# First expert table: a shorter list of candidate pairs, a fourth row buffer, and gate matrices built in groups of four from unit 40 to unit 123

## The chip, the cores and the metric

The kernel runs on one core of a Trainium2 chip. The metric is device microseconds from start to end of one execution; the median of three runs counts. The engines are TensorE (PE, matrix products; PEld is its weight load), VectorE (DVE), ScalarE (ACT), GpSimd (POOL) and SyncE (SP), which here only issues transfers. The engines run their own programs and meet at semaphores.

## The reference

One layer of a decoder: a mixer (retention and gated linear attention), then a PEER block, in which every token picks 16 experts per head out of 128 x 128 by product keys. Only the PEER block matters here:

```
s1 = einsum('thd,hnd->thn', q[:, :, 0], sub_keys1)      # 8 heads, 128 first keys
s2 = einsum('thd,hnd->thn', q[:, :, 1], sub_keys2)      # 128 second keys
v1, i1 = top_k(s1, 16)
v2, i2 = top_k(s2, 16)
cand_s = (v1[..., :, None] + v2[..., None, :]).reshape(128, 8, 256)
cand_i = (i1[..., :, None] * 128 + i2[..., None, :]).reshape(128, 8, 256)
top_s, sel = top_k(cand_s, 16)
eidx = take_along_axis(cand_i, sel, axis=-1)
gate = softmax(top_s, axis=-1)
act = gelu(einsum('thkd,td->thk', u_tab[eidx], xb))
return einsum('thk,thkd->td', gate * act, v_tab[eidx])
```

There are 512 prompt tokens and 64 sample tokens, 2048 features and 16384 experts, all in float32.

## The kernel before

The program runs stages one after the other: input projection, mixer, output projection, queries, `experts_hidden` (the first expert table, `u_tab`), `outputs` (the second table, `v_tab`), `finish`. The change touches `experts_hidden` alone, from 1506 to 2920 us of the profiled execution.

**Two ways to the experts.** 384 of the tokens (`ND`) take the dense way: the whole table goes by, one unit of 128 experts after another (`NKEYS` = 128 units of 1 MB), PE multiplies each unit with all 384 tokens (48 matmuls of 128x384, L1612 to L1614: three products for a split in two parts), ACT applies gelu (L1668) and SP stores the result to `hidden`. Which of these products count is said by gate matrices, one 128x128 matrix per token, that the next stage multiplies in. The other 192 tokens take the sparse way: for each of 192 columns (`NGATHER`) POOL gathers 128 table rows of 8 KB with an indirect transfer (L1540, 1 MB each), and DVE forms the dot products with the tokens (`dot`, L1803).

**One unit on each engine.** SP loads the unit after next (`Units.load`); it may go once `split_lo` of the unit that had this buffer is done. ACT makes the high part (`split_hi`, L1401) once PE has finished the unit before the last, DVE the low part (`split_lo`, L1405), PE multiplies. In its iteration n DVE does `split_lo(n+1)`, then one piece of routing (`route`, n < 40) or the scaled one-hot rows of the gate matrices (`firsts_hots`), then its dots.

**Routing, units 0 to 39.** The tokens form five tiles, eight units to a tile. In them DVE finds the best 16 of 128 keys for 16 lists (`best_keys`, three units), adds all 16 x 16 = 256 pairs per head (`candidates`), takes the best 16 of them with MAX8, FIND_INDEX8 and MATCH_REPLACE8 (`best_pairs`, two units; five passes over each head's list), turns the index into two positions with a shift and a mask and looks the keys up (`first_keys`, `pick`, `softmax`, two units).

**Gate matrices, units 40 to 87.** A gate matrix is the product of two 128x128 matrices of one-hot rows: POOL makes the second keys' (`hot[1]`, L1556), DVE the first keys' times the gates (`hot[0]`, L1811), PE multiplies them (L1597) after the unit's 48 matmuls, ACT copies four at a time to a staging buffer (L1653), and SP stores each 32 (`store_group`, 2 MB). Each unit makes `per_unit` = 8 of them, in two halves of `B` = 4, so that 384 are made in 48 units. There is one set of eight `hot` buffers: POOL and DVE wait until PE has made all eight of the unit before (`made`, 2m).

**Gathers.** A table of corners, `spread`, says how many gathers have been issued by which unit: 22 by unit 40, 114 by unit 88, 192 by unit 128. They start at unit 17. Three row buffers (`ROWS`) take turns, so gather g waits for dot g-3. In a unit, POOL issues the gathers first and makes `hot[1]` after them.

Of the kernel before, what the change touches and what calls it, by code (L numbers as in the profile page):

```python
# [62 lines left out]
ROWS = 3  # L63
AHEAD = 3
# [1361 lines left out]
def experts_hidden(nc, name, c, u_units, h_src, hidden, queries, keys, u_rows, h_rows, expert_ids, dots, gates0, G):  # L1426
# [17 lines left out]
    with ExitStack() as ctx:  # L1444
# [6 lines left out]
        row = [a.sb(f"row{s}", [P, D]) for s in range(ROWS)]  # L1451
# [3 lines left out]
        spare = a.sb("spare", [P, HEADS * C2])  # L1455
# [3 lines left out]
        cand_left = spare[:].rearrange("p (h n) -> p h n", n=C2)  # L1459
        picks_hot = spare[:].rearrange("p (k j) -> p k j", j=TOPK)  # L1460
        hot = [[spare[:, (2 * n + x) * P:(2 * n + x + 1) * P] for n in range(per_unit)] for x in range(2)]
# [7 lines left out]
        half = [a.sb(f"half{n}", [P, HEADS, TOPK], U32) for n in range(2)]  # L1469
# [18 lines left out]
        row_in = [a.gpsimd_dma_sem(f"row_in{s}") for s in range(ROWS)]  # L1488
# [3 lines left out]
        def _(sp):  # L1492
# [22 lines left out]
            for n in range(NKEYS):  # L1515
# [15 lines left out]
        def _(pool):  # L1531
# [3 lines left out]
            def gather(g):  # L1535

                wait(pool, row_used, g - ROWS + 1)

                pool.sem_inc(carried, 1)
                pool.indirect_dma_start(row[g % ROWS][:], None, u_rows,  # L1540
                                        bass.IndirectOffsetOnAxis(expert_ids[:, g:g + 1], 0)).then_inc(row_in[g % ROWS], 16)

            for n in range(NKEYS):
                if n == first_gate:
                    pool.wait_ge(kept, 3 * (TILES - 2))
                for g in gathers(n):
                    gather(g)
                m = n - first_gate
                if 0 <= m < ND // per_unit:

                    wait(pool, made, 2 * m)

                    pool.sem_inc(carried, 1)
                    for x in range(per_unit):
                        k = per_unit * m + x
                        nc.gpsimd.tensor_scalar(hot[1][x], iota[:], seconds[:, k:k + 1], None,  # L1556
                                                ALU.is_equal).then_inc(seconds_hot, 1)

        @block.tensor
        def _(pe):  # L1560
# [29 lines left out]
            def gate_matrices(m):  # L1590
                for y in range(2):

                    wait(pe, staged, 2 * (m - 1) + y + 1)
                    pe.wait_ge(seconds_hot, per_unit * m + B * (y + 1))
                    pe.wait_ge(firsts_hot, per_unit * m + B * (y + 1))
                    for x in range(B):
                        ins = mm(tq[y][:, x, :], hot[1][B * y + x], hot[0][B * y + x], start=True, stop=True)  # L1597
                    ins.then_inc(made, 1)
# [6 lines left out]
            for n in range(NKEYS):  # L1605
# [16 lines left out]
                if first_gate <= n < after_gates:  # L1622
                    gate_matrices(n - first_gate)

        @block.scalar
        def _(act):
# [17 lines left out]
            def stage_gates(m):  # L1644
                x, at = (m // 4) % 2, per_unit * (m % 4)
                if m % 4 == 0:

                    wait(act, g_stored[x], 16 * (m // 8))
                if m == 0:
# [597 lines left out]
```

## Time and profile before

| | us |
|---|---|
| median of 3 runs (4140.73 to 4147.33) | 4144.82 |
| the profiled execution | 4139.19 |
| its span, first to last instruction | 4137.4 |
| first table: gelu of unit 0 / unit 40 / unit 88 / unit 127 begin at | 1530.0 / 1956.8 / 2573.0 / 2916.8 |
| PE busy, of the span | 3629.7 |
| DVE busy, of the span | 2599.5 |
| POOL busy, of the span | 1261.4 |
| mean granted TensorE clock | 0.930 |

The profiled execution lies 5.6 us below the median and 1.5 us below the lowest of the three runs. Busy shares over the span are means over stages with different limits, so they say little on this stage. The beginnings of the gelus (one a unit, right after the unit's last matmul) divide the stage into units.

### The profile page before, as it was taken

How to read it: one execution, taken by the hardware profiler on the slowest of the kernel's cores; microseconds unless marked ns; L12 is line 12 of the kernel's file. 1: busy time of each engine (PE TensorE's matmuls, PEld its weight loads, DVE VectorE, ACT ScalarE, POOL GpSimd, SP SyncE). 2: the span in 40 equal slices, each digit the busy share in tenths (PEclk: the TensorE clock that was granted, in tenths of full speed). 3: DMA queues.
4: the chain of work that ended last, by engine and by line, in shares of the span. 5: the costliest groups of instructions: out<-in, count | busy, mean ns of one | idle time of the engine just before them, and what ended most of it. 6: DMA issues, size and time to landing. Idle time of an engine off the chain costs nothing. (4 is left out here: it accounts for less than half of the span.)

```text
span 4137.4 us, 49902 instructions
## 1 busy us (share of the span) xinstructions
PE 3629.7 (88%) x19469; PEld 3375.9 (82%) x19469; DVE 2599.5 (63%) x3484; ACT 1083.1 (26%) x984; POOL 1261.4 (30%) x990
## 2 busy tenths in 40 slices
PE   6999996876977969987888888999699999999996
PEld 5888885655856869877888888999699999999996
DVE  3111112883223129999766776777687888888887
ACT  3222222332112123322333333222122222222222
POOL 0000000000000000112988996333244444445441
PEclk8999997777988989998999999999899999999998
DMA  4222223534333454554777878999788898989986
GB/s 159 107 109 107 108 99 109 159 115 172 120 143 109 160 183 148 202 208 181 290 289 284 305 295 306 381 374 381 281 332 338 335 359 320 365 323 347 350 320 232
DMA packets 209787, 983.08 MB, mean 238 GB/s; under 512 B 20593, under 2 KB 84401, under 8 KB 111202
## 3 DMA queue, kind: packets, MB, share of 16 engines
q1 hardware_dynamic: 130898, 523.57, 34.1%
q0 software_dynamic: 60960, 424.18, 26.9%
q10 hardware_dynamic: 17776, 33.27, 2.2%
q8 instruction: 99, 1.62, 0.2%
q14 instruction: 54, 0.44, 0.0%
HBM read 873.43 MB, written 107.52 MB: 237 GB/s over the span
## 5 line engine op out<-in xcount | busy, mean ns | idle before, releaser
L1612 PE MATMUL hidden_hp<-hidden_dense_hi,hidden_whi 128*128 128x384 f32 x2048 | 713.2, 348 | 65.8 <-DVE hidden_wlo L1405 65.8
L2038 PE MATMUL outputs_vp<-outputs_w_hi,outputs_whi 128*128 128x384 f32 x2048 | 694.3, 339 | 81.7 <-DVE outputs_wlo L1405 41.6
L1613 PE MATMUL hidden_hp<-hidden_dense_lo,hidden_whi 128*128 128x384 f32 x2048 | 701.4, 343 | 0.0
L1614 PE MATMUL hidden_hp<-hidden_dense_hi,hidden_wlo 128*128 128x384 f32 x2048 | 700.7, 342 | 0.0
L2039 PE MATMUL outputs_vp<-outputs_w_lo,outputs_whi 128*128 128x384 f32 x2048 | 692.4, 338 | 0.0
L2040 PE MATMUL outputs_vp<-outputs_w_hi,outputs_wlo 128*128 128x384 f32 x2048 | 692.3, 338 | 0.0
L1540 POOL DMA_INDIRECT hidden_row<-u_rows,expert_ids x192 | 319.7, 1665 | 1220.6 <-DVEq L1782 713.4
L1803 DVE CUSTOM_DVE_ANT_0 hidden_row<-hidden_row,hidden_h_row 128x2048 f32<-128x2048 f32 x192 | 438.3, 2293 | 134.3 <-DMA hidden_row<-u_rows,expert_ids 133.1
L1853 POOL DMA_INDIRECT outputs_row<-v_rows,outputs_id x192 | 318.6, 1660 | 629.6 <-DVE accg L1987 572.9
L1401 ACT CAST outputs_whi<-outputs_raw 128x2048 fp32r<-128x2048 f32 x128 | 244.8, 1912 | 858.6 <-PE outputs_vp L2040 604.1
L2038 PEld LDWEIGHTS outputs_vp<-outputs_w_hi,outputs_whi 128*128 128x128 f32 x2048 | 390.9, 191 | 86.4 <-issue 78.0
L1612 PEld LDWEIGHTS hidden_hp<-hidden_dense_hi,hidden_whi 128*128 128x128 f32 x2048 | 399.6, 195 | 74.4 <-DVE hidden_wlo L1405 57.3
L1987 DVE SCALAR_TENSOR_TENSOR accg<-outputs_row,outputs_w_op,accg 128x2048 f32<-128x2048 f32 x192 | 450.5, 2347 | 3.7 <-DVE accg L1987 0.5
L1405 DVE TENSOR_TENSOR hidden_wlo<-hidden_raw,hidden_whi 128x2048 fp32r<-128x2048 f32 x128 | 296.2, 2314 | 190.6 <-ACT hidden_whi L1401 189.7
L1556 POOL TENSOR_SCALAR hidden_spare<-hidden_iota,hidden_seconds 128x128 f32<-128x128 f32 x384 | 400.7, 1057 | 7.6 <-PE hidden_tq L1597 6.1
L1613 PEld LDWEIGHTS hidden_hp<-hidden_dense_lo,hidden_whi 128*128 128x128 f32 x2048 | 398.9, 195 | 0.0
L1405 DVE TENSOR_TENSOR outputs_wlo<-outputs_raw,outputs_whi 128x2048 fp32r<-128x2048 f32 x128 | 293.1, 2290 | 167.4 <-ACT outputs_whi L1401 165.2
L1614 PEld LDWEIGHTS hidden_hp<-hidden_dense_hi,hidden_wlo 128*128 128x128 f32 x2048 | 397.3, 194 | 0.0
L2039 PEld LDWEIGHTS outputs_vp<-outputs_w_lo,outputs_whi 128*128 128x128 f32 x2048 | 390.8, 191 | 0.0
L2040 PEld LDWEIGHTS outputs_vp<-outputs_w_hi,outputs_wlo 128*128 128x128 f32 x2048 | 390.6, 191 | 0.0
L487 PE MATMUL in_proj_acc<-in_proj_whi,rows_hi 128*128 128x512 f32 x960 | 373.5, 389 | 0.0
L492 PE MATMUL in_proj_acc<-in_proj_wlo,rows_hi 128*128 128x512 f32 x768 | 298.8, 389 | 0.0
(308 smaller groups left out, 5058.9 us busy)
## 6 DMA issues: line engine op xcount, KB each, us to landing
hidden_raw<-u_units SPq DMA_DIRECT2D x128, 1024.0 KB
outputs_raw<-v_units SPq DMA_DIRECT2D x128, 1024.0 KB
w_in_raw<-w_in SPq DMA_DIRECT2D x48, 1024.0 KB, 5.5
hidden<-hidden_hid SPq DMA_DIRECT2D x128, 192.0 KB
gate_mat<-hidden_big SPq DMA_DIRECT2D x12, 2048.0 KB
outputs_w<-hidden SPq DMA_DIRECT2D x16, 1536.0 KB
outputs_g<-gate_mat SPq DMA_DIRECT2D x16, 1536.0 KB
w_out_raw<-w_out SPq DMA_DIRECT2D x16, 1024.0 KB, 6.1
```

The lines of the kernel that those rows point to most:

```text
L487: nc.tensor.matmul(acc[t][:], hi[:, kk, tok], whi[q][:, k, :], start=first, stop=False)
L1405: self.nc.vector.tensor_tensor(self.lo[s][:], self.raw[s][:], self.hi[s][:].bitcast(F32), ALU.subtract).then_inc(self.lo_done, 1)
L1540: pool.indirect_dma_start(row[g % ROWS][:], None, u_rows, bass.IndirectOffsetOnAxis(expert_ids[:, g:g + 1], 0)).then_inc(row_in[g % ROWS], 16)
L1556: nc.gpsimd.tensor_scalar(hot[1][x], iota[:], seconds[:, k:k + 1], None, ALU.is_equal).then_inc(seconds_hot, 1)
L1612: mm(o, un.hi[s][:, x, :], h_hi[:, x, :], start=x == 0, stop=False)
L1613: mm(o, un.hi[s][:, x, :], h_lo[:, x, :], start=False, stop=False)
L1614: ins = mm(o, un.lo[s][:, x, :], h_hi[:, x, :], start=False, stop=x == KT - 1)
L1803: v.tensor_tensor_reduce(r[:], r[:], h_row[g % 3 // 2][:], 1.0, 0.0, mult, ALU.add, dots[:, g:g + 1]).then_inc(row_used, 1)
L1987: v.scalar_tensor_tensor(o[:], r[:], w_op[:, j:j + 1], o[:], mult, ALU.add).then_inc(gat.row_used, 1)
L2038: mm(o, un.hi[x][:, at, :], W_hi[s][:, e, :], start=e == 0, stop=False)
L2039: mm(o, un.hi[x][:, at, :], W_lo[s][:, e, :], start=False, stop=False)
L2040: ins = mm(o, un.lo[x][:, at, :], W_hi[s][:, e, :], start=False, stop=e == CH - 1)
```

## The change

- **Candidates.** Both lists are sorted, so a pair (a, b) can be among the best 16 only if (a+1)(b+1) <= 16. The new list holds, for the first four a, all 16 b (`CW` = 64), and for the other twelve a the first four b (12 x `NARROW` = 48): `C2` = 112 instead of 256 elements per head. Two instructions build it instead of eight. The index is turned into positions by a longer piece in `first_keys`: 16 small instructions instead of 5 ahead of `pick`, with five waits instead of two.
- **Buffers.** A fourth buffer of gathered rows in this stage alone (`U_ROWS`); gather g waits for dot g-4. `spare` keeps its size and is no longer tied to the candidates'.
- **Gate matrices.** 96 groups of four are spread over units 40 to 123 (`gate_groups`): one group a unit, two in every seventh. The eight `hot` buffers become two sets of four, so POOL and DVE may build group k while PE still has to multiply group k-1. PE, ACT and DVE go by the same list. On POOL the order within a unit turns round: `hot[1]` first, then the gathers. A 2 MB store follows every seventh unit instead of every fourth.
- **Gathers.** The corner at unit 88 goes: 170 gathers are spread evenly over units 40 to 127, 1.93 a unit. Before it was 92 in 48 units (1.92), then 78 in 40 (1.95).

The diff, cut to its core:

```diff
-    HS, C2 = 2 * HEADS, TOPK * TOPK
-    B, per_unit = 4, 8
-    first_gate, after_gates = 8 * TILES, 8 * TILES + ND // per_unit
+    HS = 2 * HEADS
+    CW = WIDE * TOPK
+    C2 = CW + (TOPK - WIDE) * NARROW
+    B, groups = 4, ND // 4
+    first_gate, after_gates = 8 * TILES, NKEYS - 4
...
-        spread = [(0, 0), (17, 0), (8 * TILES, 22), (after_gates, 114), (NKEYS, NGATHER)]
+        spread = [(0, 0), (17, 0), (first_gate, 22), (NKEYS, NGATHER)]
...
+    def gate_groups(n):
+
+        if not first_gate <= n < after_gates:
+            return range(0)
+        at, of = n - first_gate, after_gates - first_gate
+        return range(groups * at // of, groups * (at + 1) // of)
...
-                done = (n - first_gate) * per_unit
-                if n > first_gate and done % GT == GT // 2 and done // GT in range(1, NG + 1):
-                    store_group(done // GT - 1)
+                for k in gate_groups(n - 2):
+                    if (k + 1) * B % GT == 0:
+                        store_group((k + 1) * B // GT - 1)
...
-                wait(pool, row_used, g - ROWS + 1)
+                wait(pool, row_used, g - U_ROWS + 1)
...
+                for k in gate_groups(n):
+
+                    wait(pool, made, k - 1)
+
+                    pool.sem_inc(carried, 1)
+                    for x in range(B):
+                        at = B * k + x
+                        nc.gpsimd.tensor_scalar(hot[1][B * (k % 2) + x], iota[:], seconds[:, at:at + 1], None,
+                                                ALU.is_equal).then_inc(seconds_hot, 1)
                 for g in gathers(n):
                     gather(g)
-                m = n - first_gate
-                if 0 <= m < ND // per_unit:
-
-                    wait(pool, made, 2 * m)
...
+            def gate_matrices(k):
+                y = k % 2
+
+                wait(pe, staged, k - 1)
+                pe.wait_ge(seconds_hot, B * (k + 1))
+                pe.wait_ge(firsts_hot, B * (k + 1))
...
-                for h in range(HEADS):
-                    d(v.tensor_tensor(cand[:, h, :].rearrange("p (a b) -> p a b", b=TOPK), bcast(pair[:, h, 0, :], 2, TOPK),
-                                      bcast(pair[:, h, 1, :], 1, TOPK), ALU.add))
+                d(v.tensor_tensor(cand[:, :, 0:CW].rearrange("p h (a b) -> p h a b", b=TOPK), bcast(pair[:, :, 0, 0:WIDE], 3, TOPK),
+                                  bcast(pair[:, :, 1, :], 2, WIDE), ALU.add))
+                d(v.tensor_tensor(cand[:, :, CW:C2].rearrange("p h (a b) -> p h a b", b=NARROW),
+                                  bcast(pair[:, :, 0, WIDE:TOPK], 3, NARROW), bcast(pair[:, :, 1, 0:NARROW], 2, TOPK - WIDE), ALU.add))
```

How it moves instructions is seen at two places. The first is POOL's row from unit 39 on, where the gate matrices begin: `hidden_spare<-hidden_iota,hidden_seconds` are POOL's one-hot matrices, `hidden_row` the gathers (the ISA row configures POOL once). Before:

```order
L1540 DMA hidden_row<-u_rows,expert_ids 128x2048 x23
L1556 ISA
L1556 TENSOR_SCALAR hidden_spare<-hidden_iota,hidden_seconds 128x128 x8
L1540 DMA hidden_row<-u_rows,expert_ids 128x2048 x2
L1556 TENSOR_SCALAR hidden_spare<-hidden_iota,hidden_seconds 128x128 x8
L1540 DMA hidden_row<-u_rows,expert_ids 128x2048 x2
```

On POOL at the same place, from unit 40 to unit 46, in the changed kernel:

```order
L1553 DMA hidden_row<-u_rows,expert_ids 128x2048 x22
L1566 ISA
L1566 TENSOR_SCALAR hidden_spare<-hidden_iota,hidden_seconds 128x128 x4
L1553 DMA hidden_row<-u_rows,expert_ids 128x2048
L1566 TENSOR_SCALAR hidden_spare<-hidden_iota,hidden_seconds 128x128 x4
...
L1566 TENSOR_SCALAR hidden_spare<-hidden_iota,hidden_seconds 128x128 x4
L1553 DMA hidden_row<-u_rows,expert_ids 128x2048 x2
L1566 TENSOR_SCALAR hidden_spare<-hidden_iota,hidden_seconds 128x128 x8
```

Four one-hot matrices stand between two pairs of gathers instead of eight (eight once in seven units), the first gather of unit 40 has moved behind the first group, and the pattern goes on to unit 123.

The second place is DVE in unit 6 of a tile, `first_keys`, between the best pairs and the first lookup (L1736, in the changed kernel L1748). `hidden_sel` is the index in the list of pairs, `hidden_halff` the two positions. Before:

```order
L1711 MAX_INDEX hidden_sel<-hidden_top,hidden_spare 128x8 x4
L1405 TENSOR_TENSOR hidden_wlo<-hidden_raw,hidden_whi 128x2048
L1748 TENSOR_TENSOR hidden_gate<-hidden_top 128x128
L1750 TENSOR_SCALAR hidden_half<-hidden_sel 128x128
L1751 TENSOR_SCALAR hidden_half<-hidden_sel 128x128
L1754 TENSOR_SCALAR hidden_halff<-hidden_half 128x128 x2
L1736 TENSOR_TENSOR hidden_spare<-hidden_halff,hidden_iota 128x2048
```

On DVE at the same place in the changed kernel:

```order
L1714 MATCH_REPLACE hidden_spare<-hidden_top,hidden_cand 128x112
L1718 MAX hidden_top<-hidden_spare 128x8 x4
L1722 MAX_INDEX hidden_sel<-hidden_top,hidden_spare 128x8 x4
L1408 TENSOR_TENSOR hidden_wlo<-hidden_raw,hidden_whi 128x2048
L1760 TENSOR_TENSOR hidden_gate<-hidden_top 128x128
L1764 TENSOR_SCALAR hidden_spare<-hidden_sel 128x128 x4
L1767 TENSOR_SCALAR hidden_spare<-hidden_spare 128x128 x4
L1770 TENSOR_SCALAR hidden_spare<-hidden_spare 128x128
L1772 TENSOR_TENSOR hidden_halff<-hidden_spare 128x128 x2
L1774 SCALAR_TENSOR_TENSOR hidden_halff<-hidden_halff,hidden_spare 128x128
L1775 TENSOR_TENSOR hidden_halff<-hidden_halff,hidden_spare 128x128
L1778 TENSOR_TENSOR hidden_halff<-hidden_halff,hidden_spare 128x128 x2
```

Eleven small instructions are added between `split_lo` of the next unit and the lookup, and the lists that the passes ahead of them read are 112 wide.

## Rows read from the trace of the kernel before

**Rows 1.** The page's first line.
```profile
span 4137.4 us, 49902 instructions
```

**Rows 2.** Busy by stretch: us, PE, PEld, DVE, ACT, POOL busy (instructions), clock, DMA share, GB/s.
```profile
1956.00:2573.00 617.00, 527.79 (x3079) 520.74 (x3078) 427.36 (x610) 206.95 (x192) 540.96 (x473) 0.93 0.78 294
2573.00:2917.00 344.00, 331.97 (x1872) 328.32 (x1870) 256.69 (x190) 90.98 (x78) 125.93 (x75) 0.99 0.97 373
```

**Rows 3.** Timeline of ACT, gelus only: start, us, instruction, [idle before, releaser].
```profile
1956.78 0.49 ACT L1668 ACTIVATE hidden_hid<-hidden_hp 128x384 f32<-128x384 f32 x1 [5.86 <-PE hidden_hp L1614]
...
2123.41 0.49 ACT L1668 ACTIVATE hidden_hid<-hidden_hp 128x384 f32<-128x384 f32 x1 [5.43 <-PE hidden_hp L1614]
2133.52 0.49 ACT L1668 ACTIVATE hidden_hid<-hidden_hp 128x384 f32<-128x384 f32 x1 [5.41 <-PE hidden_hp L1614]
...
2726.73 0.49 ACT L1668 ACTIVATE hidden_hid<-hidden_hp 128x384 f32<-128x384 f32 x1 [6.03 <-PE hidden_hp L1614]
2735.05 0.49 ACT L1668 ACTIVATE hidden_hid<-hidden_hp 128x384 f32<-128x384 f32 x1 [2.91 <-PE hidden_hp L1614]
...
2916.80 0.49 ACT L1668 ACTIVATE hidden_hid<-hidden_hp 128x384 f32<-128x384 f32 x1 [7.83 <-PE hidden_hp L1614]
```

**Rows 4.** PE groups, 1956 to 2573 us: count | busy, mean ns | idle before.
```profile
L1597 PE MATMUL hidden_tq<-hidden_spare 128*128 128x128 f32 x768 | 113.0, 300 | 89.2 <-issue 60.4 <-DVE hidden_spare L1811 16.2 <-POOL hidden_spare L1556 9.9
```

**Rows 5.** POOL groups of the same stretch, same columns.
```profile
L1556 POOL TENSOR_SCALAR hidden_spare<-hidden_iota,hidden_seconds 128x128 f32<-128x128 f32 x379 | 396.0, 1059 | 7.5 <-PE hidden_tq L1597 6.1
L1540 POOL DMA_INDIRECT hidden_row<-u_rows,expert_ids x94 | 146.6, 1559 | 63.8 <-DVE dots L1803 32.6 <-issue 16.4 <-PE hidden_tq L1597 14.7
```

**Rows 6.** One-hot matrices on POOL, same stretch: ns minimum/median/maximum, first and last start.
```profile
L1556 POOL TENSOR_SCALAR hidden_spare<-hidden_iota,hidden_seconds x379: 590/594/4724, 1954.4 to 2562.2; 128x128 f32<-128x128 f32 x190
```

**Rows 7.** Timeline of POOL in one unit.
```profile
2010.55 10.46 POOL L1556 TENSOR_SCALAR hidden_spare<-hidden_iota,hidden_seconds 128x128 f32<-128x128 f32 x8
...
2022.48 0.94 POOL L1540 DMA_INDIRECT hidden_row<-u_rows,expert_ids  x1 [0.30 <-issue]
```

**Rows 8.** Timeline of DVE beside it.
```profile
2010.53 2.56 DVE L1405 TENSOR_TENSOR hidden_wlo<-hidden_raw,hidden_whi 128x2048 fp32r<-128x2048 f32 x1 [2.12 <-ACT hidden_whi L1401]
...
2015.32 2.28 DVE L1803 CUSTOM_DVE_ANT_0 hidden_row<-hidden_row,hidden_h_row 128x2048 f32<-128x2048 f32 x1
...
2017.67 2.29 DVE L1803 CUSTOM_DVE_ANT_0 hidden_row<-hidden_row,hidden_h_row 128x2048 f32<-128x2048 f32 x1
```

**Rows 9.** Waits of PE, ACT and DVE, 2573 to 2917 us: total us, times, longest.
```profile
PE hidden_hp L1612 <- DVE hidden_wlo L1405: 11.7, 8, 2.8
...
ACT hidden_whi L1401 <- DMA hidden_raw<-u_units: 77.7, 28, 6.2
...
DVE hidden_row L1803 <- DMA hidden_row<-u_rows,expert_ids: 70.7, 41, 7.1
```

**Rows 10.** Busy by stretch (columns of rows 2), units 16 to 39.
```profile
1670.00:1935.00 265.00, 227.13 (x1245) 221.86 (x1243) 256.06 (x713) 72.30 (x79) 46.22 (x22) 0.94 0.55 207
```

**Rows 11.** Waits of PE, 1670 to 1957 us (columns of rows 9).
```profile
PE hidden_hp L1612 <- DVE hidden_wlo L1405: 35.4, 17, 3.5
PE hidden_tg L1587 <- DVE hidden_gate L1764: 11.5, 1, 11.5
```

**Rows 12.** DVE groups: a pass over 128 and over 256 elements; an add of 128x512.
```profile
L1702 DVE FIND_INDEX8 hidden_idx<-hidden_vals,hidden_big 128x8 uint32<-128x128 f32 x48 | 13.7, 286 | 0.0
...
L1702 DVE FIND_INDEX8 hidden_sel<-hidden_top,hidden_cand 128x8 uint32<-128x256 f32 x24 | 10.0, 419 | 0.0
...
L895 DVE TENSOR_TENSOR mixer_rot<-mixer_ra,mixer_rb 128x512 f32<-128x512 f32 (+1 forms) x5 | 3.5, 691 | 0.2
```

**Rows 13.** Timeline of DVE: the pairs of a tile, and its `first_keys`.
```profile
1801.29 2.77 DVE L1724 TENSOR_TENSOR hidden_cand<-hidden_vals 128x256 f32<-128x256 f32 x8
...
1833.76 0.28 DVE L1748 TENSOR_TENSOR hidden_gate<-hidden_top 128x128 f32<-128x128 f32 x1
...
1834.80 2.29 DVE L1736 TENSOR_TENSOR hidden_spare<-hidden_halff,hidden_iota 128x2048 f32<-128x2048 f32 x1
```

More of the change, by code:

```diff
@@ L63 @@
 ROWS = 3
+U_ROWS = 4
+WIDE = 4
+NARROW = TOPK // (WIDE + 1) + 1
 AHEAD = 3
@@ L1450, in experts_hidden @@
         h_row = [a.sb(f"h_row{n}", [P, D]) for n in range(2)]
-        row = [a.sb(f"row{s}", [P, D]) for s in range(ROWS)]
+        row = [a.sb(f"row{s}", [P, D]) for s in range(U_ROWS)]
         ident, iota = a.sb("ident", [P, P]), a.sb("iota", [P, P])
         big = [a.sb(f"big{n}", [P, NKEYS * GT]) for n in range(2)]
-        spare = a.sb("spare", [P, HEADS * C2])
+        spare = a.sb("spare", [P, D])
         q, kt = big[0][:, 0:D], big[0][:, D:2 * D].rearrange("p (h n) -> p h n", n=NKEYS)
@@ L1458, in experts_hidden @@
         scores_left = spare[:].rearrange("p (h n) -> p h n", n=NKEYS)
-        cand_left = spare[:].rearrange("p (h n) -> p h n", n=C2)
+        cand_left = spare[:, 0:HEADS * C2].rearrange("p (h n) -> p h n", n=C2)
         picks_hot = spare[:].rearrange("p (k j) -> p k j", j=TOPK)
-        hot = [[spare[:, (2 * n + x) * P:(2 * n + x + 1) * P] for n in range(per_unit)] for x in range(2)]
+        hot = [[spare[:, (2 * n + x) * P:(2 * n + x + 1) * P] for n in range(2 * B)] for x in range(2)]
         stage = [big[n][:].rearrange("p (a t) -> p a t", t=GT) for n in range(2)]
@@ L1468, in experts_hidden @@
         sel = a.sb("sel", [P, HEADS, TOPK], U32)
-        half = [a.sb(f"half{n}", [P, HEADS, TOPK], U32) for n in range(2)]
+        by_pick = [spare[:, n * HK:(n + 1) * HK].rearrange("p (h k) -> p h k", k=TOPK) for n in range(9)]
+        parts, partf, narrow = [x.bitcast(U32) for x in by_pick[0:4]], by_pick[4:8], by_pick[8]
         halff = [a.sb(f"halff{n}", [P, HEADS, TOPK]) for n in range(2)]
@@ L1487, in experts_hidden @@
         g_stored = [a.sem(f"g_stored{n}") for n in range(2)]
-        row_in = [a.gpsimd_dma_sem(f"row_in{s}") for s in range(ROWS)]
+        row_in = [a.gpsimd_dma_sem(f"row_in{s}") for s in range(U_ROWS)]
         block = ctx.enter_context(nc.Block())
@@ L1588, in turn_back @@
                 ins.then_inc(back, 1)
[L1590 to L1598, printed above, removed]
+            def gate_matrices(k):
[3 more added lines that the diff above has]
+                pe.wait_ge(firsts_hot, B * (k + 1))
+                for x in range(B):
+                    ins = mm(tq[y][:, x, :], hot[1][B * y + x], hot[0][B * y + x], start=True, stop=True)
+                ins.then_inc(made, 1)
             for b in range(4):
@@ L1621, in _ @@
                     turn_back(TILES - 1)
[L1622 to L1623 removed]
+                for k in gate_groups(n):
+                    gate_matrices(k)
         @block.scalar
@@ L1642, in keep, with stage_gates @@
                     nc.scalar.copy(x[:, (t - 2) * P:(t - 1) * P], tg[:, n, :]).then_inc(kept, 1)
[L1644 to L1649, printed above, removed]
+            def stage_gates(k):
+                per = GT // B
+                x, at = (k // per) % 2, B * (k % per)
+                if k % per == 0:
+                    wait(act, g_stored[x], 16 * (k // (2 * per)))
+                if k == 0:
                     act.wait_ge(found, TILES)
-                for y in range(2):
-                    act.wait_ge(made, 2 * m + y + 1)
-                    nc.scalar.copy(stage[x][:, :, at + B * y:at + B * (y + 1)].rearrange("p a t -> p t a"),
-                                   tq[y][:]).then_inc(staged, 1)
+                act.wait_ge(made, k + 1)
+                nc.scalar.copy(stage[x][:, :, at:at + B].rearrange("p a t -> p t a"), tq[k % 2][:]).then_inc(staged, 1)
             for b in range(4):
@@ L1799, in dot, with firsts_hots @@
             def dot(g):
-                vec.wait_ge(row_in[g % ROWS], 16 * (g // ROWS + 1))
-                r = row[g % ROWS]
+                vec.wait_ge(row_in[g % U_ROWS], 16 * (g // U_ROWS + 1))
+                r = row[g % U_ROWS]
                 v.tensor_tensor_reduce(r[:], r[:], h_row[g % 3 // 2][:], 1.0, 0.0, mult, ALU.add,
                                        dots[:, g:g + 1]).then_inc(row_used, 1)
-            def firsts_hots(m):
-                wait(vec, made, 2 * m)
-                for x in range(per_unit):
-                    k = per_unit * m + x
-                    v.tensor_scalar(hot[0][x], iota[:], firsts[:, k:k + 1], gates[:, k:k + 1], ALU.is_equal,
+            def firsts_hots(k):
+                wait(vec, made, k - 1)
+                for x in range(B):
+                    at = B * k + x
+                    v.tensor_scalar(hot[0][B * (k % 2) + x], iota[:], firsts[:, at:at + 1], gates[:, at:at + 1], ALU.is_equal,
                                     mult).then_inc(firsts_hot, 1)
```

34 lines of the change are left out of this document (20 added, 14 removed).

## The prediction, made before the changed kernel was run

> **What bounds the kernel now.** The change touches one stage, so I read by stretches. The span is 4137.4 us [rows 1]. First the beginnings of the gelus, which mark the units: the gelu of unit 40 begins at 1956.78, that of unit 127 at 2916.80 [rows 3], so these 87 units take 960.0 us. A unit in which nothing waits takes 10.11 us with eight gate matrices (2133.52 - 2123.41) and 8.32 us without (2735.05 - 2726.73) [rows 3]; the reader sees there that eight gate matrices cost PE 1.79 us. PE's floor for the 87 units is 87 x 8.32 + 48 x 1.79 = 810 us; 150 us are lost.
>
> Next, who loses them. In the first of the two stretches the DMA engines are busy for 0.78 of the time and the clock is 0.93; in the second, DMA 0.97 and clock 0.99 [rows 2]. The groups of PE show idle time ahead of the gate matrices of 89.2 us in the first stretch [rows 4]; most of it is put down to "issue", so the releaser has to be found elsewhere. POOL is busy for 541.0 of 617 us there [rows 2], and another 16.4 us are its own gaps [rows 5]: 557 of 617. POOL is the bound of this stretch. The rest of PE's loss there is the clock at its lower level (1.2 of 2.4 GHz) after such waits. In the last stretch nothing waits for long: PE waits 11.7 us, ACT 77.7 us for the unit loads and DVE 70.7 us for rows [rows 9]. That stretch is at the edge of the DMA engines.
>
> Why POOL is slow is in two timelines. A one-hot matrix takes 0.594 us in the median, at most 4.7 [rows 6], but eight in a row took 10.46 us [rows 7] and not 4.75. Beside them DVE ran three instructions that read two tensors, of 2.56, 2.28 and 2.29 us [rows 8]; the excess, 5.7 us, is most of their 7.1 us. So POOL stands still while DVE reads two inputs, and about one POOL instruction gets through with each. In the Trainium skill, "GPSIMD Engine Reference", section 1 (Specifications), the SBUF interfaces are shared with VectorE, with contention where VectorE has two SBUF inputs; taken as full exclusion, this is the slower rival below.
>
> Before unit 40 DVE is the bound: busy 256.1 of 265 us in units 16 to 39 [rows 10], and PE waits for it, 35.4 us at the units and 11.5 us for the last tile's gates [rows 11].
>
> **The candidates.** A pass over 256 elements takes 419 ns, over 128 286 [rows 12]: 133 ns for 128 elements, so 150 ns for the 144 that go. Five passes for each of 8 heads make 40 x 0.150 = 6.0 us a tile. The eight adds took 2.77 us [rows 13]; the two new ones are 128x512 and 128x384, each at most the 0.69 us of a 128x512 add [rows 12], together 1.2: 1.6 us saved. `first_keys` grows: five small instructions took 1834.80 - 1833.76 = 1.04 us [rows 13], 0.21 each; eleven more, with three more waits, cost 2.3 us (bounds 1.5 and 3.1 us: eleven at half and at all of the 0.28 us that one takes from its start to its end [rows 13], since their ends overlap). Net 6.0 + 1.6 - 2.3 = 5.3 us a tile. In tiles 2, 3 and 4 DVE is the bound, and a tile still needs more on DVE than the 72 us of PE, so all of it passes to the end: 3 x 5.3 = **16 us**. Bounds: 11 us (two tiles) and 20 us (a little of tile 1, and clock). Tiles 0 and 1 have PE as the bound and give nothing.
>
> **The gate matrices, work that stays.** PE's 384 matrices, POOL's and DVE's one-hots, 170 gathers and twelve stores stay; only their density changes. So each engine's need for the 87 units can be set against 960 us:
> - PE: 810 us.
> - DMA: 0.78 x 617 + 0.97 x 344 = 815 us at full use [rows 2]. At the 0.97 that the last stretch reached, 840.
> - DVE: 427 + 257 = 684 us [rows 2]. No bound.
> - POOL: in the first stretch it ran 473 instructions beside 48 splits and 93 dots, 141 two-input instructions. If each held one POOL instruction, 332 were free: 266 one-hots at 0.594 and 66 gathers at 0.94 [rows 7], 220 us. The other 141 took 541 - 220 = 321, 2.27 us each. In the changed kernel there are 554 POOL instructions beside 257: 257 x 2.27 = 583, the 297 free ones 206 x 0.594 + 91 x 0.94 = 208, gaps 16.4 x 170 / 94 = 30. Together 821 us.
>
> Spreading thus takes the peak off POOL, but leaves it, PE and the DMA engines within 4% of each other, and a transfer or a wait that comes late on one is not made up by the others. I scale by what the stretches show: POOL's stretch took 617 for 557 (x 1.11), PE's took 344 for 324 of PE's floor (x 1.06), DMA's 344 for 334 (x 1.03). So 821 x 1.11 = 911, 810 x 1.06 = 859, 815 x 1.03 = 840. The handshake that stood behind the 1.11 (POOL may only begin when PE has made all eight) is loosened by the two sets of buffers, so I lean on the other two and take **860 us**: a gain of 100. Bounds 825 and 917.
>
> A rule speaks against the lower bound: the Trainium skill, "DMA: Bandwidth & Descriptors", section "Where 436 GB/s comes from", gives HBM about 358 GB/s for one core. This case's last stretch shows 373 GB/s [rows 2], so here the row decides. By the page, as an estimate, the stretch could not be shorter than 865 us and the lower bound would be gone.
>
> **The fourth buffer and the order on POOL.** DVE waited 71 us for rows in the second stretch [rows 9]. DVE has slack in the new pattern, so the buffer is worth nothing by itself; it covers late rows. With the one-hots ahead of the gathers, a wait of POOL for `made` now stands ahead of two gathers; what it delays is DVE's dot and, behind it, the next `split_lo`. I take it at zero: the gather is issued over a unit ahead. Without that cover a late row costs up to the 7.1 us of [rows 9]. On SP each 2 MB store still stands between two unit loads, twelve times, but now where DMA is nearly full.
>
> **Sum.** 4139.2 (the profiled execution) - 16 - 100 = 4023. That execution lay 5.6 us under the median of the runs, which spread over 6.6; I add 3: **4026 us**.
>
> **The rivals.**
> - *PE alone is left as the bound.* Two sets of buffers and a fourth row buffer hide every lateness: 825 us or less for the stretch, a gain of 135 and more: 3991 or less. For it: PE's units of 8.32 us run on at DMA 0.97. Against it: DMA need 815 by itself.
> - *The stores collide with the loads.* The last stretch's pace, 344 / 39 = 8.8 us a unit, is already DMA's; if the gates' 86 us of PE and the twelve stores (2 MB at 373 GB/s, 5.6 us each, 67 us) come on top, the stretch takes 87 x 8.8 + 86 + 67 = 919 us, a gain of 41: 4082 + 3 = 4085. ACT's 77.7 us of waits for unit loads [rows 9] speak for it; that the average need still fits speaks against.
> - *Slower: POOL is shut out fully.* If at the new density no POOL instruction gets through beside a two-input one, POOL stands still for 257 x 2.28 = 586 us [rows 8] and works for 384 x 0.594 + 170 x 0.94 + 30 = 418, 1004 us in all; with the x 1.03 of the best stretch 1034: 74 us more than before, less the 16: 4200. It decides from about one in three: each instruction that gets through takes 0.7 us off the 1004, and the sum with its x 1.03 falls under 976 (before, and the 16) once 80 of 257 do. Against it: by this count the first stretch would have kept POOL busy for 141 x 2.28 + 379 x 0.594 + 94 x 0.94 = 635 us, more than its 617 and far more than 541.
> - *The change doesn't relieve POOL*, since gathers in order behind one-hots keep it waiting: its x 1.11 stays or grows, 911 to 945 us: 4077 to 4111.
>
> **How the numbers follow.** Forecast (840 to 885 us, 4006 to 4051): 0.60. PE alone, under 840: 0.13. Stores or POOL waits, 885 to 945: 0.20. Above that: 0.07, of which slower 0.04, no change 0.02. About 0.2% is what a measurement of this kernel can tell from no change. That gives faster 0.94, same 0.02, slower 0.04. The range leaves out some 0.1 at each end: 3991 (stretch 825) to 4083 (stretch 917).
>
> **What would show it.** The distance from the gelu of unit 40 to that of unit 127: 825 to 917, mostly 9.2 us units and a few of 10 to 14. DMA share about 0.95, POOL busy about 0.9. A one-hot's mean on POOL rises above 1059 ns while its median stays 594. PE's idle time ahead of gate matrices falls from 89 us to under 30, and some appears ahead of L1612 (now L1624), behind the loads. The gelu of unit 40 begins 11 to 20 us earlier. If PE still idles ahead of gate matrices, the POOL term was wrong; if ahead of units with ACT waiting for loads, the DMA term.

## The result, and the profile after

The changed kernel takes 4077.6 us in the median of 4 runs (4069.27 to 4082.67) against 4146.07 for the kernel before: 0.9838 of it, interval 0.9816 to 0.986. That is 1.6% or 68 us faster. Forecast were 4026 us and a range of 3991 to 4083. The sign and the range held; the gain is 57% of the one forecast (68 of 119 us), and the experiments show that a part that I had costed at nothing, the fourth row buffer, is worth some two thirds of it.

The profiled execution took 4075.24 us, its span is 4073.5. The beginnings of the gelus, on ACT's timeline, divide it as in [rows 3] (units 40, 46, 47, 48 and 127):

```profile
1940.17 0.49 ACT L1679 ACTIVATE hidden_hid<-hidden_hp 128x384 f32<-128x384 f32 x1 [6.91 <-PE hidden_hp L1626]
...
1995.45 0.49 ACT L1679 ACTIVATE hidden_hid<-hidden_hp 128x384 f32<-128x384 f32 x1 [5.50 <-PE hidden_hp L1626]
2005.57 0.49 ACT L1679 ACTIVATE hidden_hid<-hidden_hp 128x384 f32<-128x384 f32 x1 [5.45 <-PE hidden_hp L1626]
2023.48 0.49 ACT L1679 ACTIVATE hidden_hid<-hidden_hp 128x384 f32<-128x384 f32 x1 [6.68 <-PE hidden_hp L1626]
...
2859.32 0.49 ACT L1679 ACTIVATE hidden_hid<-hidden_hp 128x384 f32<-128x384 f32 x1 [9.19 <-PE hidden_hp L1626]
```

Unit 0's gelu begins at 1528.4 (before: 1530.0), unit 40's at 1940.2 (before: 1956.8), unit 127's at 2859.3 (before: 2916.8). So of the 63.9 us between the spans, 1.6 lie before the stage, 15 in its first 40 units, 41 in the 87 units after them (919.1 us against 960.0), and 6 in the stages behind it, which the change does not touch. Those 87 units took 919 us where I had forecast 860 and at most 917.

The busy times of those 87 units (columns of [rows 2]):

```profile
1939.00:2859.00 920.00, 844.36 (x4951) 838.47 (x4949) 680.95 (x803) 297.22 (x269) 756.84 (x545) 0.96 0.87 337
```

Before, a stretch of 617 us at DMA share 0.78 was followed by one of 344 at 0.97 [rows 2]; now it is one stretch at 0.87. Neither PE nor the DMA engines are full. Of the 109 us above PE's floor of 810, PE waits for 76 (920 - 844); for the other 33 it is busy longer than the floor, at a granted clock of 0.96. Who waits for whom (PE, POOL, DVE; total us, times, longest):

```profile
PE hidden_tq L1609 <- DVE hidden_spare L1835: 73.8, 17, 8.8
...
POOL hidden_spare L1566 <- PE hidden_tq L1609: 78.2, 41, 5.2
POOL hidden_row L1553 <- issue: 35.5, 152, 0.4
POOL hidden_row L1553 <- DVE dots L1827: 35.5, 13, 4.4
...
DVE hidden_row L1827 <- DMA hidden_row<-u_rows,expert_ids: 173.7, 81, 10.3
```

It is a ring: PE waits ahead of the gate matrices for DVE's one-hots, DVE waits for gathered rows, POOL, which issues the gathers, waits for PE's gate matrices. POOL's groups (columns of [rows 5]):

```profile
L1566 POOL TENSOR_SCALAR hidden_spare<-hidden_iota,hidden_seconds 128x128 f32<-128x128 f32 x376 | 469.4, 1261 | 80.0 <-PE hidden_tq L1609 78.2
L1553 POOL DMA_INDIRECT hidden_row<-u_rows,expert_ids x169 | 287.8, 1703 | 72.1 <-issue 35.5 <-DVE dots L1827 35.5 <-PE hidden_tq L1609 1.1
```

757 us busy, 36 of gaps, 114 of waits: POOL is working, standing still in front of DVE or waiting for 907 of 920 us. A one-hot now takes 1261 ns in the mean instead of 1059 [rows 5].

The loss has a rhythm: units of 9.2 us, one of 10.1 with two groups (unit 46's gelu to 47's, 10.12), and after it one of 13 to 21 (to 48's, 17.91); a unit is counted here from its own gelu to the next, so that its gate matrices lie in it, and this long one is unit 47. What happens there shows first on POOL (timeline):

```profile
1979.67 14.81 POOL L1566 TENSOR_SCALAR hidden_spare<-hidden_iota,hidden_seconds 128x128 f32<-128x128 f32 x8
1994.64 1.08 POOL L1553 DMA_INDIRECT hidden_row<-u_rows,expert_ids  x1 [0.16 <-issue]
1996.03 0.96 POOL L1553 DMA_INDIRECT hidden_row<-u_rows,expert_ids  x1 [0.30 <-issue]
```

then on DVE, on PE and on SP's queue:

```profile
1992.84 2.25 DVE L1835 TENSOR_SCALAR hidden_spare<-hidden_iota,hidden_firsts,hidden_gates 128x128 f32<-128x128 f32 x8
2000.53 2.29 DVE L1827 CUSTOM_DVE_ANT_0 hidden_row<-hidden_row,hidden_h_row 128x2048 f32<-128x2048 f32 x1 [5.44 <-DMA hidden_row<-u_rows,expert_ids]
...
2006.17 2.37 DVE L1827 CUSTOM_DVE_ANT_0 hidden_row<-hidden_row,hidden_h_row 128x2048 f32<-128x2048 f32 x1 [3.34 <-DMA hidden_row<-u_rows,expert_ids]
...
2010.67 1.10 DVE L1835 TENSOR_SCALAR hidden_spare<-hidden_iota,hidden_firsts,hidden_gates 128x128 f32<-128x128 f32 x4
...
2011.92 1.41 PE L1609 MATMUL hidden_tq<-hidden_spare 128*128 128x128 f32 x5 [6.39 <-DVE hidden_spare L1835]
...
2011.14 0.43 SPq L1510 DMA_DIRECT2D gate_mat<-hidden_big  x1
```

The eight one-hots of unit 46 occupy POOL for 14.81 us. Only then do the unit's two gathers go out, at 1994.64 and 1996.03. DVE has nothing to do from 1995.09 on, gets its rows at 2000.53 and 2006.17, and comes to the next group's one-hots at 2010.67. PE stands from 2005.53 to 2011.92. The 2 MB store is issued at 2011.14, when this is over. The other part of the loss is the clock, and the DMA engines are busiest where PE stands (columns of [rows 2]):

```profile
1990.00:1995.00 5.00, 5.00 (x31) 5.00 (x30) 5.00 (x11) 0.00 (x0) 4.84 (x4) 1.00 0.44 182
1995.00:2000.00 5.00, 5.00 (x37) 5.00 (x36) 0.09 (x1) 4.15 (x4) 4.50 (x7) 1.00 0.70 218
2000.00:2005.00 5.00, 5.00 (x30) 5.00 (x30) 2.30 (x2) 0.12 (x1) 4.66 (x5) 1.00 1.03 432
2005.00:2011.00 6.00, 0.53 (x4) 0.21 (x2) 4.83 (x5) 0.49 (x1) 3.71 (x4) 0.87 1.02 425
2011.00:2016.00 5.00, 4.08 (x15) 4.12 (x16) 5.00 (x6) 2.00 (x2) 2.40 (x2) 0.50 1.04 428
```

After its 6.39 us of standing PE runs at its lower clock level (0.50 of full speed in the 5 us from 2011 on), which adds some 2 us to the unit: 17.91 is 9.2, 6.4 and 2.3. While POOL is at its eight one-hots the DMA engines are half idle (0.44); the rows asked for late then move when the engines are full (1.02 to 1.04).

Before unit 40, PE's waits fell (columns of [rows 11]; there 35.4 and 11.5):

```profile
PE hidden_hp L1624 <- DVE hidden_wlo L1408: 23.0, 11, 3.5
PE hidden_tg L1599 <- DVE hidden_gate L1788: 13.8, 1, 13.8
```

### The profile page after: what moved, and what is told of

Read it like the earlier page. It is cut to its first block and busy times, and to the rows that moved or that the text cites. A ratio compares the mean times of both kernels' runs of the same rounds, so it can differ in the third digit from the quotient of the medians.

```text
span 4073.5 us, 49975 instructions
## 1 busy us (share of the span) xinstructions
PE 3608.8 (89%) x19469; PEld 3360.9 (83%) x19469; DVE 2568.2 (63%) x3509; ACT 1083.2 (27%) x984; POOL 1355.0 (33%) x990
## 5 line engine op out<-in xcount | busy, mean ns | idle before, releaser
L1624 PE MATMUL hidden_hp<-hidden_dense_hi,hidden_whi 128*128 128x384 f32 x2048 | 710.1, 347 | 42.0 <-DVE hidden_wlo L1408 41.9
L1553 POOL DMA_INDIRECT hidden_row<-u_rows,expert_ids x192 | 334.2, 1740 | 952.1 <-DVEq L1806 713.1
L1566 POOL TENSOR_SCALAR hidden_spare<-hidden_iota,hidden_seconds 128x128 f32<-128x128 f32 x384 | 476.1, 1252 | 122.9 <-PE hidden_tq L1609 78.2
L1624 PEld LDWEIGHTS hidden_hp<-hidden_dense_hi,hidden_whi 128*128 128x128 f32 x2048 | 396.2, 193 | 46.8 <-DVE hidden_wlo L1408 31.0
```

Of the source, the lines that this page charges most:

```text
L1553: pool.indirect_dma_start(row[g % U_ROWS][:], None, u_rows, bass.IndirectOffsetOnAxis(expert_ids[:, g:g + 1], 0)).then_inc(row_in[g % U_RO ...
L1566: nc.gpsimd.tensor_scalar(hot[1][B * (k % 2) + x], iota[:], seconds[:, at:at + 1], None, ALU.is_equal).then_inc(seconds_hot, 1)
L1624: mm(o, un.hi[s][:, x, :], h_hi[:, x, :], start=x == 0, stop=False)
```

## The experiments

Each ratio is to the kernel before, run on the same chip, with its 95% interval; the "units" column is the distance from the gelu of unit 40 to that of unit 127 in the profiled execution.

| kernel | median us | ratio | units, us |
|---|---|---|---|
| before | 4146.07 | 1 | 960.0 |
| the change | 4077.6 | 0.9838 (0.9816 to 0.986) | 919.1 |
| late_store | 4104.14 | 0.9922 (0.9891 to 0.9952) | 951.4 |
| gathers_first | 4062.72 | 0.9811 (0.9767 to 0.9855) | 906.0 |
| second_on_dve | 4087.28 | 0.9876 (0.9845 to 0.9907) | 926.5 |
| three_rows | 4123.19 | 0.9971 (0.9952 to 0.999) | 955.7 |
| cands_only | 4128.37 | 0.9971 (0.9954 to 0.9987) | 947.9 |
| cands_rows4 | 4083.94 | 0.9874 (0.9843 to 0.9905) | 915.3 |
| all_on_dve | 4011.87 | 0.9698 (0.9668 to 0.9729) | 854.4 |
| split_store | 4079.72 | 0.9859 (0.9829 to 0.9888) | 907.8 |
| all_dve_dense | 3984.09 | 0.9634 (0.9604 to 0.9663) | 823.9 |
| all_dve_rows3 | 4047.88 | 0.9779 (0.9748 to 0.981) | 876.2 |
| pool_takes_second | 4031.72 | 0.9747 (0.9717 to 0.9777) | 871.7 |
| all_on_dve_split | 3986.2 | 0.9636 (0.9605 to 0.9666) | 826.6 |

The kernels were run in four groups (the change; the next four rows of the table after it; the four from cands_only to split_store, and the last four). The kernel before had the medians 4146.07, 4140.33, 4138.78 and 4138.43 beside them, so a difference of medians across groups is good to some 8 us: the change against three_rows is 46 us by the medians and 55 by the ratios, against all_on_dve 66 and 58. The profiled executions of cands_only (4111.75), three_rows (4110.48), cands_rows4 (4071.9) and split_store (4069.54) lie 17, 13, 12 and 10 us under the medians of their kernels, so their last column is on the low side.

### Is it the store? late_store

```diff
-                for k in gate_groups(n - 2):
+                for k in gate_groups(n - 4):
```

> The changed kernel with one edit: each 2 MB store of gate matrices is issued two units later. In the changed kernel PE loses 5 to 12 us in the unit after each unit with two groups (the first of them in unit 47), 74 us in all. Theory A: the loss comes from POOL, whose eight one-hot matrices in the unit with two groups stand ahead of that unit's gathers, so the rows reach DVE late; the store only happens to be near. Then the long units stay where they are (47, 54, 61, ...) and the time stays within 4065 to 4090 us. Theory B: the store takes the DMA engines from the gathers; then the long units move by two (49, 56, 63, ...).

It took 26 us more, outside A's range. Some of the long units after the units with two groups stayed (47: 17 us, 68: 17, 75: 14), and new ones came up to three units behind the store, which now goes out in units 49, 56 and 63 (52: 16, 58: 17, 63: 17). PE idled 95 us ahead of gate matrices, POOL waited longer for PE (total us, times, longest):

```profile
PE hidden_tq L1609 <- DVE hidden_spare L1835: 95.2, 27, 7.9
...
POOL hidden_spare L1566 <- PE hidden_tq L1609: 111.2, 37, 9.5
```

Neither theory alone: the unit with two groups costs by itself, as A says, and a store elsewhere costs too. In the change the two fall together. Why that is cheaper is not shown: the DMA engines are already full again (1.02) in the 6 us before the store.

### POOL's order: gathers_first

```diff
             for n in range(NKEYS):
+                for g in gathers(n):
+                    gather(g)
                 for k in gate_groups(n):
...
-                for g in gathers(n):
-                    gather(g)
```

> The changed kernel with POOL's old order: a unit's gathers ahead of its one-hot matrices. Theory A (the late gathers behind eight one-hots): the gathers are issued one unit's group earlier, PE's 74 us of idle time ahead of gate matrices falls to 20 to 50, the time to 4030 to 4060 us. Theory B (stores): no change, 4078 within 10 us. Theory C (POOL as a whole has too much to do, in whatever order): idle time ahead of gate matrices stays 60 to 90 us, but the releaser changes from DVE to POOL; the time is 4065 to 4095.

4062.72 us: the medians differ by 15, the intervals overlap. The waits moved as expected of A, and of C as well (PE, POOL, DVE):

```profile
PE hidden_tq L1609 <- DVE hidden_spare L1835: 32.0, 9, 6.1
PE hidden_tq L1609 <- issue: 28.6, 12, 4.6
...
POOL hidden_spare L1568 <- PE hidden_tq L1609: 0.4, 1, 0.4
...
DVE hidden_row L1827 <- DMA hidden_row<-u_rows,expert_ids: 64.4, 46, 7.5
```

POOL's 78 us of waiting for PE are gone and DVE's waits for rows fell from 165 (the change from 1945 to 2850 us) to 64, but PE still idles 63 us ahead of the gate matrices, half of it now with POOL's one-hots as what comes last: the view puts 28.6 us down to "issue", but in each of these waits POOL's last one-hot ended 0.1 us before PE began, and DVE's had been done for 2.7 us or more. POOL was busy for 801 of 905 us. The order is a small part, 15 us by the medians and 11 by the ratios; POOL's load is the larger one.

### The unit with two groups: second_on_dve

```diff
                 for k in gate_groups(n):
+                    if k in second:
+                        continue
                     wait(pool, made, k - 1)
...
+                    if k in second:
+                        v.tensor_scalar(hot[1][B * (k % 2) + x], iota[:], seconds[:, at:at + 1], None,
+                                        ALU.is_equal).then_inc(firsts_hot, 1)
```

> The changed kernel with the second group of each unit with two groups made wholly by DVE (both one-hots, 12 x 4 more small instructions on DVE, 48 fewer on POOL). Theory A: the unit with two groups is no longer long on POOL, so the long units after it vanish: PE idle time ahead of gate matrices under 30 us, 4020 to 4050 us. Theory B (stores): the long units stay, 4070 to 4085 us.

Theory A falls in this form: 4087.28 us, no better than the change. The long units did not vanish but moved one or two units on (49, 56, 63, 70), behind the store, which goes out in units 47, 54 and 61, and POOL, with 48 fewer one-hots, only waited longer for PE (111.8 us). Relieving one place of the ring let it close at the next one. That B's store is the cause here is not shown either.

### The fourth buffer: three_rows, cands_only, cands_rows4

three_rows is the change with one figure undone:

```diff
-U_ROWS = 4
+U_ROWS = 3
```

> The changed kernel with three row buffers instead of four. I took the fourth buffer at zero by itself, as cover for late rows. Under theory A the rows are late because POOL issues them late, and in the units with two groups the fourth buffer changes little: 4075 to 4095 us. If the landing of the rows is what is late (DMA engines), three buffers cost more in every unit: 4100 to 4140 us.

4123.19 us: the second reading held, and the fourth buffer is worth 46 us here by the medians. With three, POOL is held by the dots and DVE by the rows (1945 to 2850 us):

```profile
POOL hidden_row L1553 <- DVE dots L1827: 114.8, 28, 7.4
...
DVE hidden_row L1827 <- DMA hidden_row<-u_rows,expert_ids: 230.0, 110, 10.1
```

cands_only is the kernel before with the new `candidates` and `first_keys`, and cands_rows4 is that with `U_ROWS = 4` in this stage; gate matrices stay at eight a unit in 48 units.

> The kernel before with the short list of candidate pairs alone. By the sum of the prediction DVE saves 5.3 us a tile in three tiles and all of it passes to the end: 16 us, so 0.9961 of before; the gelu of unit 40 begins 11 to 20 us earlier and the 87 units after it still take 960 us within 10. If the DVE time were given back in the gate units, the ratio would be 1.00.

> The kernel before with the short list and the fourth row buffer, gate matrices still eight a unit in 48 units (with the long list the fourth buffer does not fit into SBUF, so it can't be tried alone). Prediction: the fourth buffer by itself is worth 0 to 10 us beyond the short list, since POOL's handshake bounds the gate units: 0.994 to 0.996 of before. Rival, after the run with three buffers, which lost 46 us: the fourth buffer is the part that pays, and here too: 0.985 to 0.990.

cands_only: 0.9971, 12 us (5 to 19 by the interval), where the sum had 16; of the 40 units before the gates 13.8 us are gone in its trace. cands_rows4: 0.9874, the medians 44 us lower. The rival was right, and not the prediction. The place is POOL's wait in the gate units, where the gather stands ahead of the eight one-hots, in cands_only and then in cands_rows4 (1945 to 2565 us):

```profile
POOL hidden_row L1545 <- DVE dots L1821: 61.8, 16, 8.4
```
```profile
POOL hidden_row L1546 <- DVE dots L1822: 20.4, 5, 7.9
```

41 us less waiting on the engine that bounds the stretch; units 41 to 88 took 581 us instead of 610.

cands_rows4 also gives what the spread itself brought: the change is cands_rows4 plus the spread (with its two sets of buffers and POOL's turned order), 0.9838 against 0.9874, 6 us by the medians, 15 by the ratios, and the intervals overlap. With three buffers (three_rows against cands_only) it is 5 us by the medians, and the ratios are the same.

### POOL out of the ring: all_on_dve

```diff
-                for k in gate_groups(n):
-
-                    wait(pool, made, k - 1)
...
-                        nc.gpsimd.tensor_scalar(hot[1][B * (k % 2) + x], iota[:], seconds[:, at:at + 1], None,
-                                                ALU.is_equal).then_inc(seconds_hot, 1)
...
+                    v.tensor_scalar(hot[1][B * (k % 2) + x], iota[:], seconds[:, at:at + 1], None,
+                                    ALU.is_equal).then_inc(firsts_hot, 1)
```

> The changed kernel with all one-hot matrices made by DVE, so that POOL only gathers and never waits for PE. Theory now: POOL's order is what costs, since each gather stands behind four one-hots that wait for PE's matrices and for DVE's two-input instructions, and DVE, PE and POOL wait for each other in a ring. Then DVE's waits for rows fall from 165 us to under 80 in spite of 111 us more work on DVE, PE's idle time ahead of gate matrices under 35 us, time 4000 to 4045 us. Rival: the DMA engines deliver the rows late whatever POOL does; then DVE still waits over 120 us and the time stays at 4065 to 4100.

4011.87 us, 66 less than the change, though DVE has more to do. Busy times and waits (PE, POOL, DVE):

```profile
1945.00:2765.00 820.00, 788.21 (x4745) 784.73 (x4744) 718.12 (x1166) 291.11 (x261) 342.31 (x161) 0.99 0.95 361
```
```profile
PE hidden_tq L1599 <- DVE hidden_spare L1827: 31.8, 12, 4.8
...
POOL hidden_row L1553 <- DVE dots L1817: 461.1, 86, 12.8
...
DVE hidden_row L1817 <- DMA hidden_row<-u_rows,expert_ids: 9.2, 13, 2.0
```

DVE hardly waits for rows any more: POOL is always there when a buffer comes free. Between the beginning of a gather on POOL and the beginning of its dot lie, from the 26th gather on, 17.0 us in the mean of this trace, 11.1 in the change's, 12.6 in that of cands_rows4 and 10.8 before. The lead includes the dot's own waits, but the landing does not explain it: from issue to landing a row takes 9.2 us here and 9.8 in the change in the median. With three buffers (three_rows) the lead is 9.8 us, so in the change POOL came too late to make full use of the fourth buffer. The rival (rows late by the DMA engines whatever POOL does) is out.

### What the spread is worth then: all_dve_dense, all_dve_rows3

all_dve_dense is cands_rows4 with the same edit as all_on_dve.

> The short list and the fourth buffer with gate matrices eight a unit in 48 units as before, but all one-hots made by DVE, so POOL only gathers: the other half of the run in which DVE made them with the spread (4012 us). It tells what the spread itself is worth once POOL is out of the way. DVE then needs 2.2 + 16 x 0.24 + 1.92 x 2.3 = 10.5 us in a gate unit, about PE's 10.1. Theory (POOL's ring ate the gain of the spread): still a loss here against 4012, 10 to 40 us, since DVE and PE peak together in 48 units: 4025 to 4055 us. Rival (the spread never mattered, taking the one-hots off POOL is all): 4005 to 4020 us.

Both expectations were wrong. Eight gate matrices a unit in 48 units with POOL out is the fastest kernel of all, 3984.09 us, 28 less than the same with the spread. The DVE time on which the expectation rested was about right: in the 48 gate units it is busy 481 of 495 us, 10.0 us a unit, and a one-hot takes 0.28 to 0.35 us. But it does not hold PE up: the units take 10.3 us, and PE waits 2.2 us in all ahead of gate matrices (the first row is the stretch from 1945 to 2765 us, the others are DVE's groups from 1945 to 2440):

```profile
1945.00:2765.00 820.00, 814.12 (x4921) 809.77 (x4920) 736.33 (x1175) 301.26 (x268) 314.37 (x166) 1.00 0.96 375
```
```profile
L1819 DVE TENSOR_SCALAR hidden_spare<-hidden_iota,hidden_firsts,hidden_gates 128x128 f32<-128x128 f32 x376 | 131.6, 351 | 0.0
...
L1821 DVE TENSOR_SCALAR hidden_spare<-hidden_iota,hidden_seconds 128x128 f32<-128x128 f32 x376 | 104.2, 277 | 0.0
```

The 87 units take 823.9 us against PE's floor of 810. With POOL in the ring the spread was worth 5 and 6 us; with POOL out it costs 28.

> The kernel in which DVE makes all one-hots, spread as in the change, with three row buffers instead of four. With POOL in the ring the fourth buffer was worth 46 us (4123 against 4078). If it is worth that because it covers gathers that POOL issues late, it is worth little once POOL is free: 4012 to 4030 us. If it covers the time a row takes to land, it is worth 30 us or more here too: 4040 to 4070 us.

36 us more than with four buffers: the second reading was the right one, and it holds whether POOL is in the ring or not. With three buffers DVE waits 65 us for rows instead of 9, though POOL has no other work: the buffer covers the time that a row takes to land.

### The stores: split_store, all_on_dve_split, pool_takes_second

```diff
-                sp.dma_start(G[g], stage[x]).then_inc(g_stored[x], 16)
+                keys_of = slice(*((0, 48), (48, 96), (96, 128))[j])
+                sp.dma_start(G[g][:, keys_of, :], stage[x][:, keys_of, :]).then_inc(g_stored[x], 16)
```

(one part in each of three successive units.)

> The changed kernel with each 2 MB store cut into three parts in three successive units. If the burst of a store on the DMA engines is part of the loss (late stores alone cost 26 us, in new long units), cutting it gives 10 to 30 us: 4048 to 4068. If the place of the store was good because the late gathers leave the DMA engines free just then, cutting it moves part of it into busy units: 4078 to 4100 us.

> The kernel in which DVE makes all one-hots, with each 2 MB store cut into three parts in three units. Its long units (12 to 16 us) come right when the store is issued. If the burst of the store is their cause, now that rows are early, this takes 5 to 20 us off 4012; if DVE's row is, nothing: 4008 to 4018 us.

> As the kernel in which DVE makes all one-hots, but in a unit with two groups POOL makes the second group's second one-hots, behind that unit's gathers: 48 of 384 on POOL. In the run with all on DVE, PE idled 32 us ahead of gate matrices, in the unit after each with two groups, where DVE had 16 small instructions at once. If the length of DVE's row there is the cause, this takes 5 to 15 us off: 3998 to 4008 us. If the four one-hots block POOL's next gathers as in the change, it is lost again: 4015 to 4040 us.

Cut stores do nothing for the change (4079.72 us) and 26 us for the kernel with POOL out (3986.2 against 4011.87), more than the 20 expected. How a store costs there is seen on ACT, DVE and PE behind the store of unit 47 (issued at 2006.84):

```profile
2030.30 1.91 ACT L1404 CAST hidden_whi<-hidden_raw 128x2048 fp32r<-128x2048 f32 x1 [4.42 <-DMA hidden_raw<-u_units]
2032.25 2.29 DVE L1408 TENSOR_TENSOR hidden_wlo<-hidden_raw,hidden_whi 128x2048 fp32r<-128x2048 f32 x1 [4.41 <-ACT hidden_whi L1404]
2036.50 2.04 PE L1599 MATMUL hidden_tq<-hidden_spare 128*128 128x128 f32 x8 [3.43 <-DVE hidden_spare L1827]
```

The next unit load, issued at 2015.58, has landed only after 14.7 us (6.8 in the median), so ACT's and DVE's split and DVE's one-hots come late too. This comes back every seventh unit: ACT waits 2.3 to 5.7 us for a load in units 49, 56 and so on to 119, two behind each store, and PE waits in units 50, 57 and so on to 120. With the stores cut, PE's idle time ahead of gate matrices fell from 31.8 us to

```profile
PE hidden_tq L1601 <- DVE hidden_spare L1829: 10.7, 10, 2.7
```

So once rows are early, what is left of the spread's loss is the burst of 2 MB ahead of the next unit's load on SP's queue. The burst alone does not do it: all_dve_dense has the same twelve stores whole, in units of 10.3 us, and PE hardly waits. The dense kernel with cut stores was not run.

pool_takes_second (48 one-hots back on POOL, behind the gathers) took 4031.72: 20 us lost again by an eighth of the second keys' one-hots. The number is in the second reading's range, but its reason fails: DVE waited only 1.6 us for rows, so the gathers were not late. POOL waited 71 us for PE, PE waited 37 us for DVE's one-hots instead of 32, and in the 87 units PE was busy for 834 us instead of 823, at a granted clock of 0.97 instead of 0.99. What delays DVE there stays open.

## Why the total fell in the range and the reasons did not hold

- **The total.** The stretch of 919 us lies above the bound of 917. 4139.2 - 15 - 41 is 4083, the very end of the range; another 8 us that I had not forecast, 1.6 ahead of the stage and 6.4 behind it, brought the profiled execution to 4075. That the total fell inside the range is in part luck.
- **Candidates, 16 us.** Held: 12 us alone (interval 5 to 19), 15 us in the change by the gelus of units 0 and 40.
- **The four needs.** PE 810 and the DMA engines 815 stand; all_dve_dense came within 14 us of PE's. In the change PE's waits brought the lower clock with them: 76 us of waits and 33 us of longer matmuls. POOL was put at 821 with its gaps; it measured 757 + 36 = 793. That count, one POOL instruction through per two-input instruction of DVE, was 4% too high.
- **The step that failed** is the choice of 860 us for the stretch. POOL's own scale (x 1.11) gave 911, and I set it aside because "the handshake that stood behind the 1.11 ... is loosened by the two sets of buffers". It was not what stood behind it: in [rows 5] POOL waits 32.6 us for dots and only 20.8 for PE. In the changed kernel the waits for dots are 35.5 us and those for PE rose to 79: a group may be built one group ahead, but in order, and the gathers now stand behind it. The stretch took 919 us. The rival "the change doesn't relieve POOL" had 911 to 945 and its reason ("gathers in order behind one-hots keep it waiting"), at 0.20 together with the stores.
- **"I take it at zero"** failed twice. The fourth buffer was worth 44 us by itself, by the time a row takes to land and by POOL's wait for dots in [rows 5], which I had read and not priced. And POOL's turned order was not free: "the gather is issued over a unit ahead" held in units with one group and not in those with two. Turned back it gave 15 us by the medians (gathers_first). Of the 100 us that I gave to the spread, 6 are left within the intervals, and the order is not the whole reason: with POOL out of the ring the spread cost 28.
- **The store rival** gave 919 us for the stretch, and 919 was measured, but that is a coincidence: cutting the stores in the change moved nothing. They do cost in other kernels (late_store, all_on_dve).
- **Full exclusion** did not occur: POOL was busy for 757 us, not 974.
- **The signs.** PE's idle time ahead of gate matrices stayed at 74 us (89 before), with DVE as releaser. By the prediction's last sentence that says that the POOL term was wrong, and it was. The DMA share of 0.87, not 0.95, and POOL's busy share of 0.82, not 0.9, say the same. The idle time that I had put ahead of L1624, behind the loads, is 1.9 us. The one-hot on POOL did what I expected: mean 1261 ns, median 607.
- **HBM's 358 GB/s.** The Trainium skill, "DMA: Bandwidth & Descriptors", section "Where 436 GB/s comes from", would have kept the stretch at 865 us or more, by my estimate. all_dve_dense moved 375 GB/s through 820 us and took 824 for the stretch, so on this chip, with one core at work, the row decides.

## What to carry to other kernels

Count what an in-order engine must do next to what it must issue: a gather that stands behind computation which itself waits for the engine that needs the gather closes a ring, and spreading the work leaves the ring as it is. Price each wait of the bounding engine by its releaser before choosing which scale to drop. When one part of a change frees memory and another uses it, cost the buffer by its own waits; here it was worth 44 us of a gain of 68.

## What the runs showed of the hardware

- A one-hot of 128x128 costs 1.26 us on POOL beside DVE's two-input instructions (mean; 0.607 in the median; a few take up to 4.8, two such instructions long) and 0.28 on DVE. Moving 384 of them to DVE, which then was busy for 741 us of the stretch instead of 681, made the kernel faster by 66 us (all_on_dve against the change) and 100 us (all_dve_dense against cands_rows4).
- 0.96 busy DMA engines and a PE that is busy for 814 of 820 us go together over 820 us, at a granted clock of 1.00. I had scaled the needs up by 3% and more for their meeting.
- A row gather of 1 MB takes 5.6 to 16.7 us from issue to landing in the change, 9.8 in the median. With a mean lead of 17 us from issue to use DVE waits 9 us in all (all_on_dve), with 11 it waits 174 (the change).
- A 2 MB store ahead of a 1 MB load on one queue held ACT up for as much as 5.7 us where a unit takes 9.2 us (all_on_dve), and did not hold PE up where it takes 10.3 (all_dve_dense).
